# Gate projections of a hybrid decoder step by one level of Strassen's scheme: seven block products for eight

## The chip, the cores and the metric

The kernel runs on one core of one Trainium2 chip. The metric is the device time of one execution in microseconds. Three runs of the kernel before took 2144.91, 2146.51 and 2146.85 us; the median is 2146.51 us.

## The reference

One layer of a decoder for a prompt of 2048 tokens and 8 sample rows (together 2056 columns, `TT`), in float32, with `D_MODEL` 1024:

```python
h = (rms_norm(x, norm_g) * (1.0 + scale) + shift)
proj = h @ w_in                       # columns: q, k, v (1536 each), z_a, u_b, z_b (512 each), g_a, g_b (1024 each)
...                                   # dilated window attention on q, k, v -> a; trailing means of u_b -> p
ya = (a * jax.nn.silu(z_a)) @ w_a_out
yb = (p * jax.nn.silu(z_b)) @ w_b_out
m = jax.nn.sigmoid(g_a) * ya + jax.nn.sigmoid(g_b) * yb
return x + gate * (m @ w_out)
```

The change concerns `g_a` and `g_b`: 2048 of the projection's columns over all 2056 tokens, with a contraction of 1024.

## The kernel before

Float32 accuracy is had with three matmuls where one would do (`three_pass`, L755 to L763): each operand is split into a high part, rounded to TensorE's format, and a low part, the rest; high by high, high by low and low by high are added up in PSUM. Rounding is a copy (a cast on GpSimd or an activation on ScalarE), the low part a subtraction on VectorE.

The program has three stages that follow each other on TensorE: attention with its projections (`attend`, up to about 1160 us), the remaining projections (`finish`), and the outputs (`combine`, from 1764.4 us). The normalised input `h` lies transposed in SBUF as `hH` and `hL`, eight k blocks of 128 rows by 2056 tokens.

`finish` projects 26 tiles of 128 output columns. A tile is five chunks of 412 tokens (the last 408), each of 8 k blocks times 3 matmuls (`project`). Tiles 0 to 7 are u_b and z_b in pairs; between them VectorE makes the window sums (`windows`, L419) and TensorE the pooling matmul of each chunk (`pooled`). Tiles 8 and 9 are z_a, tiles 10 to 25 the gates: `g_a` is eight tiles, `g_b` eight. The weights of a tile are 512 KB, loaded by SyncE (L266) into one of two buffers, rounded by GpSimd (`split_hi`, L381) and subtracted by VectorE (`split_lo`, L397), each at the start of the tile ahead. ScalarE takes every chunk out of PSUM through a Sigmoid (L559) and stores it to `gT_dram`. The work of the 8 sample rows on their cached keys and values runs beside the gate tiles on VectorE: `score` (L453, L455) during tiles 10 to 17, `weigh` (L463) with `values` on TensorE during tiles 20 to 23. The last two tiles are done chunk by chunk in turn (`last`), and beside them the first inputs and weights of `combine` are fetched, rounded and subtracted (`end` on each engine).

`combine` works on 256 tokens at a time: eight branch products (`c_pa`, 256 columns per matmul, two groups of 12), multiplied by the gates on VectorE (L1942, L1944, L1946), then two output products of 512 columns (`c_py`). Its weights come in five pieces by output column (`pieces`, L1790); ScalarE rounds a piece (L1880), VectorE subtracts (L1978), and TensorE waits ahead of a branch product only for the pieces that it reads.

Order is written out by hand. Every engine runs its list in order and waits on semaphores; SyncE's list holds nearly all loads, and its DMAs go out in the order of the list. `wait_ge(proj_done, ...)` waits for a chunk's last matmul, `wait_ge(w_lo, ...)` for a tile's low part.

## Time and profile before

| | |
|---|---|
| median of the runs | 2146.51 us |
| span of the profiled execution | 2144.5 us |
| its own time | not listed apart; the median is 2.0 us above its span |
| TensorE busy | 2099.0 us (98%) |
| VectorE, ScalarE, GpSimd busy | 890.0, 616.0, 243.7 us |
| the sixteen gate tiles | 1398.6 to 1764.4 us |

A busy time is a sum of the instructions' durations without overlap. TensorE's matmuls overlap each other, so the mean duration of one is longer than the distance between two starts. The granted clock in the tables of stretches is a share of full speed. Where a line number is that of a helper (L760 to L762 are the three matmuls of `three_pass`), the names of the tiles tell the use.

### The profile page before, as it was taken

How to read it: one execution, taken by the hardware profiler on the slowest of the kernel's cores; microseconds unless marked ns; L12 is line 12 of the kernel's file. 1: busy time of each engine (PE TensorE's matmuls, PEld its weight loads, DVE VectorE, ACT ScalarE, POOL GpSimd, SP SyncE). 2: the span in 40 equal slices, each digit the busy share in tenths (PEclk: the TensorE clock that was granted, in tenths of full speed). 3: DMA queues.
4: the chain of work that ended last, by engine and by line, in shares of the span. 5: the costliest groups of instructions: out<-in, count | busy, mean ns of one | idle time of the engine just before them, and what ended most of it. 6: DMA issues, size and time to landing. Idle time of an engine off the chain costs nothing.

```text
span 2144.5 us, 36997 instructions
## 1 busy us (share of the span) xinstructions
PE 2099.0 (98%) x12759; PEld 2003.2 (93%) x12759; DVE 890.0 (42%) x2408; ACT 616.0 (29%) x2165; POOL 243.7 (11%) x389
## 2 busy tenths in 40 slices
PE   5999999999999999999999999999999999999999
PEld 3889999999999999999999999999999998998897
DVE  3543333334444344444431244132131247666664
ACT  4634333333333333333354111111121141111010
POOL 2222112111111121111100000000000000000000
PEclk9999999999999999999999999999999999999999
DMA  9756666664645646455244244255422356444441
GB/s 344 256 160 199 221 198 203 207 204 151 201 152 184 196 146 193 151 178 182 89 116 133 83 153 143 94 196 187 152 97 93 126 197 233 169 144 134 149 131 60
DMA packets 258633, 354.05 MB, mean 165 GB/s; under 512 B 24964, under 2 KB 230868, under 8 KB 257069
## 3 DMA queue, kind: packets, MB, share of 16 engines
q1 hardware_dynamic: 209849, 309.82, 43.9%
q10 hardware_dynamic: 48636, 42.33, 6.2%
q8 instruction: 84, 1.38, 0.3%
q14 instruction: 64, 0.52, 0.1%
HBM read 256.52 MB, written 183.77 MB: 205 GB/s over the span
## 4 chain that ended last, share of the span: by engine, by line
PE 92%; DVE 3%; SPq 2%; issue 1%; DMA 1%; ACT 1%; POOL 1%; ACTq 0%; DVEq 0%
PE a_pp L762 13%; PE a_pp L760 13%; PE a_pp L761 12%; PE pp L760 9%; PE pp L762 9%; PE pp L761 9%; PE c_pa L761 3%; PE c_pa L762 3%; PE c_pa L760 3%; PE c_py L761 3%; PE c_py L762 3%; PE c_py L760 2%; PE po L1598 2%; PE pqk L1564 1%; PE po L1597 1%
## 5 line engine op out<-in xcount | busy, mean ns | idle before, releaser
L760 PE MATMUL a_pp<-a_wH,hH 128*128 128x384 f32 x1520 | 528.5, 348 | 6.0 <-DVE qkv L1399 5.2
L762 PE MATMUL a_pp<-a_wH,hL 128*128 128x384 f32 x1520 | 516.2, 340 | 0.0
L761 PE MATMUL a_pp<-a_wL,hH 128*128 128x384 f32 x1520 | 514.2, 338 | 0.0
L760 PE MATMUL pp<-hH,next_H 128*128 128x412 f32 (+1 forms) x1040 | 369.9, 356 | 1.4 <-issue 1.4
L762 PE MATMUL pp<-hH,next_L 128*128 128x412 f32 (+1 forms) x1040 | 363.2, 349 | 0.0
L761 PE MATMUL pp<-hL,next_H 128*128 128x412 f32 (+1 forms) x1040 | 363.1, 349 | 0.0
L760 PEld LDWEIGHTS a_pp<-a_wH,hH 128*128 128x128 f32 x1520 | 287.1, 189 | 10.1 <-ACT qkv L1283 4.4
L761 PEld LDWEIGHTS a_pp<-a_wL,hH 128*128 128x128 f32 x1520 | 287.3, 189 | 0.0
L762 PEld LDWEIGHTS a_pp<-a_wH,hL 128*128 128x128 f32 x1520 | 286.2, 188 | 0.0
L1277 ACT ACTIVATE a_junk<-a_pp 128x128 f32<-128x128 f32 x384 | 106.6, 278 | 545.1 <-PE a_pp L762 539.0
L1388 DVE TENSOR_SCALAR a_ms<-a_ss 128x2 f32<-128x2 f32 (+1 forms) x204 | 34.5, 169 | 524.5 <-ACT a_junk L1277 524.4
L1185 POOL TENSOR_TENSOR a_rs<-a_ms,a_mhalf 128x2 f32<-128x2 f32 (+1 forms) x204 | 140.5, 689 | 842.0 <-DVE a_ms L1388 842.0
L760 PEld LDWEIGHTS pp<-hH,next_H 128*128 128x128 f32 x1040 | 195.6, 188 | 8.6 <-issue 8.1
L761 PEld LDWEIGHTS pp<-hL,next_H 128*128 128x128 f32 x1040 | 195.5, 188 | 3.8 <-issue 3.1
L762 PEld LDWEIGHTS pp<-hH,next_L 128*128 128x128 f32 x1040 | 195.3, 188 | 0.4
L761 PE MATMUL c_pa<-abL,m_wH 128*128 128x256 f32 (+1 forms) x512 | 144.4, 282 | 0.0
L762 PE MATMUL c_pa<-abH,m_wL 128*128 128x256 f32 (+1 forms) x512 | 144.0, 281 | 0.0
L760 PE MATMUL c_pa<-abH,m_wH 128*128 128x256 f32 (+1 forms) x512 | 143.6, 280 | 0.0
L1399 DVE SCALAR_TENSOR_TENSOR qkv<-a_pp,a_rs,gains 128x128 f32<-128x128 f32 x384 | 117.1, 347 | 63.3 <-POOL a_rs L1185 63.2
L559 ACT ACTIVATE ost<-pp 128x412 f32<-128x412 f32 (+1 forms) x80 | 41.3, 516 | 291.1 <-PE pp L762 291.1
L397 DVE TENSOR_TENSOR next_L<-next_st,next_H 128x1024 fp32r<-128x1024 f32 x24 | 29.4, 1224 | 215.3 <-POOL next_H L381 215.3
L1297 ACT ACTIVATE sm<-sm,nm 128x128 f32<-128x128 f32 (+1 forms) x192 | 89.0, 463 | 63.7 <-DVE nm L1420 63.5
(259 smaller groups left out, 3158.2 us busy)
## 6 DMA issues: line engine op xcount, KB each, us to landing
out_dram<-in_state_kv_w_dram SPq DMA_DIRECT2D x64, 1023.5 KB, 5.9
qkv_dram<-qkv SPq DMA_DIRECT2D x192, 192.0 KB, 2.1
qkv_in<-qkv_dram SPq DMA_DIRECT2D x192, 192.0 KB, 2.6
a_wst<-in_w_in_dram SPq DMA_DIRECT2D x38, 512.0 KB, 7.3
gl<-gT_dram SPq DMA_DIRECT2D x64, 264.0 KB, 3.9
out_dram<-in_state_kv_w_dram SPq DMA_DIRECT2D x8, 2044.0 KB, 11.3
gT_dram<-ost ACTq DMA_DIRECT2D x72, 206.0 KB, 2.6
next_st<-in_w_in_dram SPq DMA_DIRECT2D x26, 512.0 KB, 5.6
```

The costliest lines, as they stand in the source:

```text
L397: nc.vector.tensor_tensor(wL[slot], wst[slot], wH[slot].bitcast(F32), ALU.subtract).then_inc(w_lo, 1)
L559: nc.scalar.activation(out, pp[c][:, 0:width(c)], func).then_inc(evac, 1)
L760: nc.tensor.matmul(out, sH, mH, start=(i == 0), stop=False)
L761: nc.tensor.matmul(out, sH, mL, start=False, stop=False)
L762: last = nc.tensor.matmul(out, sL, mH, start=False, stop=(i == len(terms) - 1))
L1185: nc.gpsimd.tensor_tensor(rs[0:rows, s % 2, :], ms[0:rows, s % 2, :], mhalf[0:rows, :], ALU.pow).then_inc(powered, 1)
L1277: nc.scalar.activation(junk[0:rows, :], src[0:rows, i * P:(i + 1) * P], ACT.Square, accum_out=ss[0:rows, s % 2, i:i + 1]).then_inc(squared, 1)
L1297: nc.scalar.activation(sm[:, j % RP, lo:], sm[:, j % RP, lo:], ACT.Exp, bias=nm[:, j % RP:j % RP + 1], accum_out=ot[:, j % RO, E:E + 1]).t ...
L1388: nc.vector.tensor_scalar(ms[0:rows, s % 2, :], ss[0:rows, s % 2, :], 1.0 / E, EPS, ALU.mult, ALU.add).then_inc(meaned, 1)
L1399: done = nc.vector.scalar_tensor_tensor(qkv[0:rows, s % RS, i, :], src[0:rows, i * P:(i + 1) * P], rs[0:rows, s % 2, i:i + 1], gains[0:row ...
L1564: nc.tensor.transpose(pqk[:, 0:P], qkv_in[:, j % RIN, 0, :], ident[:, :])
L1598: nc.tensor.matmul(po[j % 2][:, 0:E], prT[:, j % RP, half(own(j))], qkv_in[:, j % RIN, 2, :], start=not prev, stop=True).then_inc(pv_done, 1)
```

## The change

The product of the gates' weights and `h` is cut once in each direction. Of the weights the two halves are `g_a` and `g_b` (for the same eight f tiles) and the two halves of k; of `h` they are the halves of k and two neighbouring quarters of the tokens (514 columns). Seven products of sums of blocks replace the eight products of blocks, in the form with 15 additions. There are two passes, one for each pair of quarters, and eight steps (f tiles) in each: 16 steps `s` of 7 products `i`. A product is 4 k blocks, 3 matmuls each, over 514 tokens in two halves of 258 columns (two of them twice) in two PSUM banks; three such pairs of banks are used in turn.

- The sums of `h` blocks (T1 to T4) are made once, on GpSimd, in eight units during the pooling tiles (`token_sums`), stored to `comb_dram`, and read back into places of `hH` and `hL` that the pass doesn't need. ScalarE rounds them, VectorE subtracts. Blocks that the second pass needs and the first overwrites are stored to `kept_dram` and read back (`install`).
- The sums of weight blocks are made anew in each step (`weight_sums`): four loads of 256 KB, four GpSimd operations of 512 columns, seven casts, seven subtractions. `w4` has one buffer.
- The outputs are seven additions of 516 columns on VectorE, out of PSUM, and one copy and four Sigmoids on ScalarE, then four stores a step.
- z_a is projected in twelve chunks of 344 or 340 tokens, the upper half of the tokens first.
- The sample rows' work is written into the steps. The weights of `combine` come in eight pieces of 514 columns and half of k; the first four must be ready before its first branch product.

```diff
+    PAIRS, ZA, NF = 4, 2, 10
...
+    QW, SW, HK = TT // 4, 258, KT // 2
...
+    PASSES, GP, NP = 2, KT, 7
+    GS = PASSES * GP
+    K1, K2 = 1, 0
...
+    REGIONS = (((K1, 0), (0, 2), (K2, 0), (0, 3), (1, 2), (1, 3), (K2, 1)),
+               ((K1, 0), (1, 1), (K2, 0), (0, 2), (0, 3), (1, 2), (1, 3)))
+    MADE = {1: T2, 3: T3, 4: T1, 5: T4}
+    KEPT = {0: (K1, 2), 2: (K2, 2), 6: (K2, 3)}
+    UNITS = PASSES * HK
...
+            w4 = sb("w4", [P, NP, HK, P])
+            aH = sb("aH", [P, NP, HK, P], F32R)
+            aL = sb("aL", [P, NP, HK, P], F32R)
+            bank = ps2("g_bank", [P, 6, 512])
...
+        RAW = {0: 0, 2: 1, 3: 2, 5: 3, 4: 4, 1: 5, 6: 6}
+        raw_of = lambda i: w4[:, RAW[i], :, :]
+        u1, u2, u3 = (sums[:, i, :, :] for i in range(3))
+        u4 = u1
...
+        SAW = {1: 1, 2: 2, 3: 3, 4: 5, 5: 6, 6: 7}
+        OUT_OF = {2: 0, 4: 1, 5: 2, 6: 3}
...
+            return (NP * s + i + 2) % 3
...
             def _(sp):
...
+                def store_made(unit):
+                    p, k = divmod(unit, HK)
+                    for n, (which, buf) in enumerate(((T3, 3), (T1, 0), (T2, 1), (T4, 2))):
+                        sp.wait_ge(made_ready, unit * 4 + n + 1)
+                        sp.dma_start(comb_dram[p, which, :, k, :], made[buf][:, :]).then_inc(made_stored, 16)
...
+                def gate_weights(s):
+                    f = s % GP
+                    if s:
+                        sp.wait_ge(g_lo, NP * s)
+                    for i, (c0, kh) in enumerate(((CGA, K1), (CGA, K2), (CGB, K1), (CGB, K2))):
+                        sp.dma_start(w4[:, i, :, :], w_in_v[:, kh * HK:(kh + 1) * HK, c0 + f * P:c0 + (f + 1) * P]).then_inc(g_landed, 16)
+                def install(p, i):
+                    if i in MADE:
+                        sp.dma_start(raw_region(REGIONS[p][i]), comb_dram[p, MADE[i]]).then_inc(t_landed[i], 16)
+                    else:
+                        for part in range(2):
+                            sp.dma_start(as_f32(part, REGIONS[p][i]), kept_dram[i, part]).then_inc(t_landed[i], 16)
...
+                    for s in range(GS):
+                        if s + 1 < GS:
+                            gate_weights(s + 1)
+                        if s + 1 < NS:
+                            keys(s + 1)
+                        if s < NS:
+                            shifted_copy(sp, v, 0, s, bulk)
...
+                        if s == GP - 3:
+                            install(1, 1)
+                        if s == GP - 1:
+                            for i, freed in ((0, 0), (3, 1), (2, 2), (4, 3), (5, 4), (6, 5)):
+                                sp.wait_ge(g_done, NP * s + freed + 1)
+                                install(1, i)
+                        if s == GP:
+                            sp.wait_ge(scored, NS * GROUPS)
+                            for b in range(2):
+                                values(b)
+                            sp.wait_ge(g_done, NP * GP)
+                            load_weights(0)
...
+                        if s == GS - 1:
+                            for i in range(2):
+                                sp.wait_ge(b_stored[i], 16 * PAIRS * NBC // 2)
+                            sp.wait_ge(g_lo, NP * GS)
+                            branch_inputs(0)
+                            for i in range(4):
+                                sp.wait_ge(g_stored[i], 16 * GP)
+                            gates(0, range(4))
+                            for n in range(1, NP + 1):
+                                sp.wait_ge(g_done, NP * s + n)
+                                load_weights(n)
...
             def _(pool):
...
+                def token_sums(unit):
+                    p, k = divmod(unit, HK)
+                    hi = lambda kh, th: hH[:, kh * HK + k, (2 * p + th) * QW:(2 * p + th + 1) * QW].bitcast(F32)
+                    lo = lambda kh, th: hL[:, kh * HK + k, (2 * p + th) * QW:(2 * p + th + 1) * QW].bitcast(F32)
...
+                    if unit:
+                        pool.wait_ge(made_stored, 16 * 4 * unit)
+                    nc.gpsimd.tensor_tensor(d, hi(K2, 1), hi(K1, 1), ALU.subtract)
+                    chained(nc.gpsimd.tensor_tensor(a, lo(K2, 1), lo(K1, 1), ALU.subtract))
+                    nc.gpsimd.tensor_tensor(d, d, a, ALU.add).then_inc(made_ready, 1)
+                    pool.wait_ge(made_ready, unit * 4 + 1)
...
+                    nc.gpsimd.tensor_tensor(c, c, lo(K2, 0), ALU.add).then_inc(made_ready, 1)
...
+                def weight_sums(s):
+                    pool.wait_ge(g_landed, 64 * (s + 1))
+                    if s:
+                        pool.wait_ge(g_lo, NP * s)
+                    nc.gpsimd.tensor_tensor(w4[:, 4, :, :], w4[:, 2, :, :], w4[:, 3, :, :], ALU.add).then_inc(g_sum, 1)
+                    pool.wait_ge(g_sum, 4 * s + 1)
+                    nc.gpsimd.tensor_tensor(w4[:, 2, :, :], w4[:, 0, :, :], w4[:, 2, :, :], ALU.subtract).then_inc(g_sum, 1)
+                    nc.gpsimd.tensor_tensor(w4[:, 5, :, :], w4[:, 4, :, :], w4[:, 0, :, :], ALU.subtract).then_inc(g_sum, 1)
+                    pool.wait_ge(g_sum, 4 * s + 3)
+                    nc.gpsimd.tensor_tensor(w4[:, 6, :, :], w4[:, 1, :, :], w4[:, 5, :, :], ALU.subtract).then_inc(g_sum, 1)
+                    pool.wait_ge(g_sum, 4 * s + 4)
+                def weight_hi(s, i):
+                    if s:
+                        pool.wait_ge(g_done, NP * (s - 1) + i + 1)
+                    nc.gpsimd.tensor_copy(aH[:, i, :, :], raw_of(i)).then_inc(g_hi, 1)
...
+                for n in range(2, NF):
+                    token_sums(n - 2)
...
+                    split_hi(n, n % 2)
+                for s in range(GS):
+                    weight_sums(s)
+                    for i in range(NP):
+                        weight_hi(s, i)
...
             def _(dve):
...
+                def weight_lo(s, i):
+                    dve.wait_ge(g_hi, NP * s + i + 1)
+                    nc.vector.tensor_tensor(aL[:, i, :, :], raw_of(i), aH[:, i, :, :].bitcast(F32), ALU.subtract).then_inc(g_lo, 1)
...
+                def after_product(s, i):
+                    if i == 0:
+                        return
+                    here = product_of(s, i)
+                    dve.wait_ge(g_done, NP * s + i + 1)
+                    if s and i in OUT_OF:
+                        dve.wait_ge(g_stored[OUT_OF[i]], 16 * s)
+                    if i == 1:
+                        dve.wait_ge(act_saw, s + 1)
+                        nc.vector.tensor_tensor(u2, here, u1, ALU.add).then_inc(dve_saw, 1)
+                    if i == 2:
+                        nc.vector.tensor_tensor(out_2(0), here, u1, ALU.add).then_inc(dve_saw, 1)
+                    if i == 3:
+                        dve.wait_ge(dve_saw, SUMS * s + 1)
+                        nc.vector.tensor_tensor(u3, here, u2, ALU.add).then_inc(dve_saw, 1)
+                    if i == 4:
+                        dve.wait_ge(dve_saw, SUMS * s + 3)
+                        nc.vector.tensor_tensor(out_2(1), here, u3, ALU.add).then_inc(dve_saw, 1)
+                        nc.vector.tensor_tensor(u4, here, u2, ALU.add).then_inc(dve_saw, 1)
+                    if i == 5:
+                        nc.vector.tensor_tensor(out_2(2), here, u3, ALU.add).then_inc(dve_saw, 1)
+                    if i == 6:
+                        dve.wait_ge(dve_saw, SUMS * s + 5)
+                        nc.vector.tensor_tensor(out_2(3), here, u4, ALU.add).then_inc(dve_saw, 1)
...
+                    for s in range(GS):
+                        for i in range(NP):
+                            after_product(s, i)
+                            if s < NS and i < GROUPS:
+                                score(s, i)
...
+                            if s == GS - 1:
+                                if i == 1:
+                                    pooling_lo()
...
+                                if i == 3:
+                                    gate_a(1)
+                                    weights_lo(1)
+                                if i == 4:
+                                    attention_lo()
+                                    weights_lo(2)
+                                if i == 5:
+                                    weights_lo(3)
+                            if s + 1 < GS and i >= 3:
+                                for n in range(0 if i == 3 else i, i + 1):
+                                    weight_lo(s + 1, n)
...
             def _(act):
...
+                def after_product(s, i):
+                    p, f = divmod(s, GP)
+                    if i == 0:
+                        act.wait_ge(g_done, NP * s + 1)
+                        if s:
+                            act.wait_ge(dve_saw, SUMS * s)
+                        nc.scalar.activation(u1, product_of(s, i), ACT.Copy).then_inc(act_saw, 1)
+                    if i in OUT_OF:
+                        n = OUT_OF[i]
+                        act.wait_ge(dve_saw, SUMS * s + SUM_OF_OUT[i])
+                        nc.scalar.activation(out_2(n), out_2(n), ACT.Sigmoid).then_inc(g_made, 1)
+                        act.wait_ge(g_made, 4 * s + n + 1)
+                        row, quarter = ((4, 0), (12, 1), (12, 0), (4, 1))[n]
+                        store(n, row + f, 2 * p + quarter)
...
+                            if s == GS - 1:
+                                if i == 1:
+                                    pooling_hi()
+                                if 2 <= i < 5:
+                                    weights_hi(i - 1)
+                                if i == 4:
+                                    attention_hi()
...
             def _(pe):
...
+                def product(s, i):
+                    p = s // GP
+                    if s == 0 and i < 2:
+                        pe.wait_ge(evac, after(Z0 + ZN - 3 + 2 * i))
+                    before = NP * s + i - 3
+                    if before >= 0:
+                        s0, i0 = divmod(before, NP)
+                        if i0:
+                            pe.wait_ge(dve_saw, SUMS * s0 + SAW[i0])
+                        else:
+                            pe.wait_ge(act_saw, s0 + 1)
+                    pe.wait_ge(g_lo, NP * s + i + 1)
+                    if s % GP == 0:
+                        if i in MADE:
+                            pe.wait_ge(t_lo, made_count(p, i))
+                        elif p:
+                            pe.wait_ge(t_landed[i], 32)
+                    rH, rL = region(hH, REGIONS[p][i]), region(hL, REGIONS[p][i])
+                    for j in range(2):
+                        cols = slice(j * (QW - SW), j * (QW - SW) + SW)
+                        done = three_pass(nc, bank[:, 2 * place(s, i) + j, 0:SW],
+                                          [(aH[:, i, k, :], aL[:, i, k, :], rH[:, k, cols], rL[:, k, cols]) for k in range(HK)])
+                    done.then_inc(g_done, 1)
...
+        pieces = ((0, 1), (1, 0), (1, 1), (0, 0), (0, 2), (0, 3), (1, 2), (1, 3))
+        BRANCH_PIECES, OUT_PIECES = 4, (7, 8)
+        LATE_HI, LATE_LO = {1: 4, 3: 5, 4: 6, 5: 7}, {1: 4, 3: 5, 5: 6, KT - 1: 7}
...
+                kh, th = pieces[n]
+                w = (w_a, w_b)[kh] if th < 2 else w_o[:, kh * HK:(kh + 1) * HK, :]
+                start = th % 2 * QW
+                sp.dma_start(piece(w_raw, n), w[:, :, start:min(start + QW, D)]).then_inc(cw_landed[n], 16)
...
-                    pe.wait_ge(cw_lo, piece_of((f + 1) * P - 1) + 1)
+                    pe.wait_ge(cw_lo, BRANCH_PIECES)
```

## Rows read from the trace of the kernel before

**Rows 1.** The page: span, and busy time of each engine

```profile
span 2144.5 us, 36997 instructions
PE 2099.0 (98%) x12759; PEld 2003.2 (93%) x12759; DVE 890.0 (42%) x2408; ACT 616.0 (29%) x2165; POOL 243.7 (11%) x389
```

**Rows 2.** Busy per engine by stretch, then clock, DMA share, GB/s

```profile
1398.60:1764.40 365.80, 365.80 (x1958) 359.56 (x1956) 109.89 (x149) 77.41 (x110) 15.56 (x15) 1.00 0.46 152
```

**Rows 3.** Timeline of TensorE, 412 columns, first and 43rd: start, duration

```profile
1399.28 0.35 PE L760 MATMUL pp<-hH,next_H 128*128 128x412 f32 x1
...
1407.12 0.35 PE L760 MATMUL pp<-hH,next_H 128*128 128x412 f32 x1
```

**Rows 4.** Timeline of TensorE, 256 columns, first, and the 193rd matmul

```profile
1904.50 0.28 PE L760 MATMUL c_pa<-abH,m_wH 128*128 128x256 f32 x1
...
1927.16 0.40 PE L760 MATMUL c_py<-m_wH,mH 128*128 128x512 f32 x1
```

**Rows 5.** Groups by line of GpSimd: count, busy us, mean ns, idle before

```profile
L1185 POOL TENSOR_TENSOR a_rs<-a_ms,a_mhalf 128x2 f32<-128x2 f32 x192 | 132.3, 689 | 791.4 <-DVE a_ms L1388 791.4
L1180 POOL CAST a_wH<-a_wst 128x384 fp32r<-128x384 f32 x96 | 51.1, 539 | 11.4 <-DMA a_wst<-in_w_in_dram 11.4
L381 POOL CAST next_H<-next_st 128x1024 fp32r<-128x1024 f32 x24 | 25.4, 1057 | 527.8 <-PE pp L762 461.7 <-DMA next_st<-in_w_in_dram 66.1
```

**Rows 6.** Groups by line of VectorE

```profile
L1942 DVE TENSOR_TENSOR gm<-c_pa,gl 128x512 f32<-128x512 f32 x56 | 38.5, 687 | 24.6 <-PE c_pa L762 24.6
L453 DVE TENSOR_TENSOR prod<-kt,qb 128x512 f32<-128x512 f32 x24 | 16.6, 691 | 14.2 <-DMA qb<-samp_dram 13.7
L1978 DVE TENSOR_TENSOR m_wL<-m_raw,m_wH 128x3072 fp32r<-128x3072 f32 x4 | 13.4, 3352 | 0.0
...
L419 DVE TENSOR_TENSOR run<-run 128x2061 f32<-128x2061 f32 x3 | 6.9, 2306 | 0.1
```

**Rows 7.** DMA issues: count, KB each, median us from issue to landing

```profile
out_dram<-in_state_kv_w_dram SPq DMA_DIRECT2D x8, 2044.0 KB, 11.3
...
m_raw<-in_w_a_out_dram SPq DMA_DIRECT2D x1, 512.0 KB, 3.9
m_raw<-in_w_b_out_dram SPq DMA_DIRECT2D x1, 512.0 KB, 5.4
```

**Rows 8.** Timeline of SyncE's queue: start and duration of the two issues

```profile
1745.72 0.37 SPq L1790 DMA_DIRECT2D m_raw<-in_w_a_out_dram  x1
1746.13 0.51 SPq L1790 DMA_DIRECT2D m_raw<-in_w_b_out_dram  x1
```

**Rows 9.** Timeline of GpSimd: the seven casts of bl, the first two

```profile
1789.42 5.12 POOL L1824 CAST abH<-bl 128x1056 fp32r<-128x1056 f32 x1 [71.14 <-DMA bl<-bT_dram]
1836.10 1.07 POOL L1824 CAST abH<-bl 128x1056 fp32r<-128x1056 f32 x1 [41.56 <-PE c_pa L762]
```

**Rows 10.** Timeline of VectorE beside these casts, and one subtraction without

```profile
1789.19 4.42 DVE L1978 TENSOR_TENSOR m_wL<-m_raw,m_wH 128x4096 fp32r<-128x4096 f32 x1
...
1793.73 0.83 DVE L737 TENSOR_TENSOR cw<-ol,cw 128x12 f32<-128x12 f32 x1
...
1836.72 0.72 DVE L1946 TENSOR_TENSOR mL<-m,mH 128x256 fp32r<-128x256 f32 x1 [0.48 <-ACT mH L1857]
...
1866.25 0.43 DVE L1946 TENSOR_TENSOR mL<-m,mH 128x256 fp32r<-128x256 f32 x1 [0.48 <-ACT mH L1857]
```

**Rows 11.** Busy by stretch, two stretches with full DMA queues

```profile
1381.00:1385.00 4.00, 4.00 (x24) 3.99 (x23) 0.00 (x0) 0.42 (x1) 0.00 (x0) 1.00 1.04 404
1747.00:1753.00 6.00, 6.00 (x34) 5.99 (x33) 3.22 (x1) 3.02 (x2) 0.00 (x0) 1.00 0.99 324
```

**Rows 12.** Groups by line of ScalarE

```profile
L1880 ACT ACTIVATE m_wH<-m_raw 128x3072 fp32r<-128x3072 f32 x4 | 11.1, 2768 | 0.8 <-ACT ost L595 0.8
L1847 ACT ACTIVATE abH<-a 128x1056 fp32r<-128x1056 f32 x8 | 8.7, 1090 | 92.0 <-DVE a L1920 92.0
```

671 lines of the change are left out of this document (374 added, 297 removed).

## The prediction

> **What bounds the kernel now.** I read the page's first lines, then the table of busy time by stretch, then the timeline of TensorE. TensorE is busy for 2099.0 of 2144.5 us [rows 1]. The stretch that the change rewrites, the sixteen gate tiles, lasts 365.8 us, and TensorE is busy in all of it at a granted clock of 1.00; VectorE has 110 us of work there, ScalarE 77, GpSimd 16 [rows 2]. So only TensorE's work counts there today, and the other engines have room, but room on average: what matters below is how long a chain through them takes.
>
> Of one matmul the profile's duration (349 ns for 412 columns) is not the price, since neighbours overlap; the price is the distance of the starts. With 412 columns 42 matmuls start within 7.84 us, 186.7 ns each [rows 3]. With 256 columns 192 start within 22.66 us, 118.0 ns each [rows 4]. That is 0.453 and 0.461 ns a column: a narrow matmul is hardly dearer per column, and weight loading does not set the pace. Between the two rows a column costs 0.440 ns, so 258 columns are 118.9 ns.
>
> **TensorE's own work.** Removed: 16 tiles x 5 chunks x 24 matmuls = 1920, of which 1536 have 412 columns and 384 have 408 (185.0 ns): 286.8 + 71.0 = 357.8 us. The other 8.0 us of the stretch are the samples' value matmuls, transposes and their seams, and stay. Added: 16 steps x 7 products x 24 matmuls = 2688 of 258 columns: 319.6 us. Gain 38.2 us if nothing waits. The two tiles of z_a become twelve chunks of 344 or 340 columns, 288 matmuls instead of 240: 45.0 against 44.7 us, a loss of 0.3.
>
> **The pooling stage.** GpSimd gets eight units of ten two-input operations of 514 columns, and SyncE 15 MB of stores. A tile of TensorE is 120 matmuls, 22.4 us. At the price taken below a unit is 10 x 1.3 + waits = 14 us, beside one cast of 1.06 [rows 5], and fits. VectorE's window sums of the last pair, five of 2.3 us [rows 6], meet those operations; they have one tile and one chunk (27 us) before the pooling matmul wants them, so some 14 us of slack for at most 14 us of blocking. I take 0; were GpSimd's operation above 2 us, TensorE would wait here too. In the z_a chunks four blocks of 1.05 MB come in, rounded by ScalarE and VectorE; there are 22 us for it and I take 0.
>
> **The loop of the gate steps.** This is the term that decides. One step is 7 x 2.853 = 20.0 us of TensorE. The weights of the next step have one raw buffer (w4), freed only by the last low part of the step before. So each step has a closed loop, none of it on TensorE:
> - SyncE issues four loads of 256 KB. The trace has no such group; two loads of 512 KB, issued 0.41 us apart, land 3.9 and 5.4 us after their issues [rows 7, 8], so 1 MB is there after 5.8 us. Taken 5.9.
> - GpSimd makes four sums of 512 columns. The trace has no large two-input operation of GpSimd. From below: a cast, 539 ns for 384 columns and 1057 for 1024 [rows 5], so 0.64 for 512. From above: reading two operands at the cast's 0.81 ns per column and operand (0.83), on the 0.69 of its two-column operation [rows 5]: 1.52. I take 1.3, nearer the upper row, because the reading of both operands has to be paid and only the fixed part is in doubt. Four with three waits on itself: 5.5.
> - The first cast 0.64, then at product 3 VectorE's first four low parts, each against a cast. Here the two engines block each other: VectorE's subtraction of 4.42 us began at 1789.19, GpSimd's cast at 1789.42 took 5.12 instead of 1.07 and ended 0.93 after it; VectorE's 128x12 operation behind it took 0.83 [rows 9, 10]. In reverse a 0.43 us subtraction took 0.72 beside a cast [rows 9, 10]. So a pair costs 0.45 + 0.55 = 1.0, four of them 4.0, without blocking 2.5.
> - Only then do both sums of product 4 come, 0.69 each [rows 6], which the first product of the next step waits for (it reuses that bank): 1.4.
> - Before the buffer is free: low part, sum, low part, sum, low part: 3.2. Some ten semaphore hops: 0.6.
>
> Together 5.9 + 5.5 + 4.6 + 1.4 + 3.2 + 0.6 = 21.2 us, against 20.0 of TensorE. TensorE then waits 1.2 us once a step, ahead of product 0.
>
> The Trainium skill speaks against the change here. Its "SBUF — State Buffer", section "Who interferes with whom", says that a VectorE instruction with two SBUF inputs and a GpSimd instruction that reads SBUF exclude each other; by that rule, the trace agrees with 5.12 against 1.07. Its "GPSIMD Engine Reference", section "Elementwise — side-by-side cycle accounting", gives 4497 ns for a two-input addition of 2048 columns; scaled to 512 with the cast's fixed part, my estimate is 1.3 us, and the loop would be the same 21.2; no run here shows that price yet.
>
> **Fifteen seams between steps.**
> - Into step 1: its load starts behind six loads of keys: 2.
> - Into steps 2 to 8, seven times 1.2: 8.4.
> - Into step 9: in step 7 the queue carries step 8's weights (1.0 MB), a state copy of 0.5 MB read and written (2.8 us from 11.3 for 2 MB [rows 7]), nine blocks of 1.05 MB for the second pass, three stores of 0.26 MB, then step 9's weights: 12.3 MB at the 324 to 404 GB/s that full queues move [rows 11], 34 + 2.8 us from 4.5 us into step 7. They land 20 us into step 8; then 5.5 + 4.6 + 1.4 + 0.6. Step 9 starts at 32 instead of 20: 12.
> - Into steps 10 to 14: the weighing of values, five two-input operations of 0.69 [rows 6], runs up to twice a step on VectorE and blocks GpSimd's sums, and value matmuls wait for their loads: 2.5 each, 12.5.
> - Into step 15: two group sums of about 5 us with their exponentials stand before the low parts: 6.
>
> Sum 40.9. The stretch becomes 319.6 + 8.0 + 40.9 = 368.5 against 365.8: +2.7.
>
> **Into the last stage.** Before, TensorE passed from the gates to the branch matmuls without a gap, as the output weights came in column pieces. Now the first branch matmul needs four whole pieces. In step 15 SyncE issues 2.1 MB of inputs, then pieces 1 to 3 (3.1 MB): 5.2 MB in 15 us from 3 on, the third there at 18. ScalarE rounds it in 1.9 (2.77 for 3072 columns [rows 12]) and only then the attention rows, 1.09 [rows 12]; VectorE follows with 1.25, a low part of 2.3 (3.35 for 3072 [rows 6]), a sum 0.7 and the last low part 2.3. That is 28, and TensorE is done at 20: 8. It cannot be below 0, and 12 if the queues move the lower rate of rows 11. Inside the last stage VectorE starts late but the four banks cover it: 0.
>
> Sum against the profiled execution: 2144.5 + 2.7 + 0.3 + 8 = 2155.5. The median of the runs is 2146.5, 2.0 above the span; with these 2157.5, taken as **2157 us**.
>
> **Rivals.**
> 1. The loop fits. Its condition is a GpSimd sum near the cast, 0.64, or no blocking. Then 5.9 + 2.9 + 3.2 + 1.4 + 3.2 + 0.6 = 17.2, hidden. The queue at the pass change still costs 8, the value steps 3, the group sums 3, the end 8: 2146.5 - 38.2 + 0.3 + 22 = 2131. For it: the average load is far below the span. Against: the blocking in [rows 9, 10]. If these 22 are hidden too: 2109.
> 2. The loop is longer. GpSimd's sum at 1.52 and landings 1 us later, since ScalarE's four stores per step share the queues: +1.9 a seam, 28 in all: 2185. For it: landings of the trace grow with what is in flight. Above 2 us GpSimd would also bound the pooling stage.
> 3. The forecast, which ends slower; the first rival ends faster. The point between them is a loop of 20.0: at a sum of 1.0 the plain steps no longer wait, and 1.2 less at each of the fourteen later seams brings the time to 2141; the time of before is met near 1.1.
>
> **Chances.** Forecast 0.52, first rival 0.27, all hidden 0.05, longer loop 0.16. A run tells 0.2% (4.3 us): faster, below 2142.2, is 0.32 with the first two and the edge of the loop; between, 0.13, are sums of 1.0 to 1.15; slower 0.55. The likeliest case's own range is 2147 to 2170. For 8 in 10: 2125, just under the first rival, to 2187.
>
> **What would show it.** Right: starts of product 0 are 21 to 22 us apart in steps 2 to 8, with a wait on VectorE ahead of it; GpSimd's 128x512 sums at 1.2 to 1.4; step 8 lasts over 30; TensorE idles 6 to 12 us before the first branch matmul. Wrong: steps of 20.0, with only seams 8 and 14 wider (first rival); steps above 23 (second); matmuls of 258 columns more than 121 ns apart, which [rows 4] speak against; or waits in the pooling stage.

## The result, and the profile after

The changed kernel takes 2218.81 us (four runs, 2215.34 to 2221.21) against 2145.71 us of the kernel before on the same chip: ratio 1.0339, 95% interval 1.0325 to 1.0354. The forecast was 2157, with 2125 to 2187 for the range: the direction was right, the size was not.

First the page of the kernel after; the rows answer to [rows 1].

```profile
span 2216.9 us, 38614 instructions
PE 2097.0 (95%) x13575; PEld 1992.0 (90%) x13575; DVE 1084.0 (49%) x2627; ACT 624.2 (28%) x2166; POOL 522.2 (24%) x629
```

TensorE is busy only 2.0 us less than before, though 38 us of matmuls were to be saved, and the span is 72.4 us longer: part of its matmuls ran at a lower clock, and there is idle time. The table of stretches says where. Columns: stretch, its length, busy of PE, PEld, DVE, ACT, POOL with their instructions, granted clock, DMA share, GB/s. It answers to [rows 2]; below it two single steps.

```profile
1397.20:1834.90 437.70, 362.86 (x2723) 349.00 (x2721) 273.73 (x357) 78.10 (x104) 171.38 (x165) 0.92 0.65 179
1477.05:1503.67 26.62, 21.94 (x167) 21.74 (x166) 14.95 (x21) 3.15 (x6) 10.89 (x11) 0.87 0.62 164
1503.67:1525.87 22.20, 21.01 (x176) 20.81 (x175) 13.81 (x20) 3.14 (x6) 10.89 (x11) 1.00 0.72 183
```

The stretch of the gates, up to the first branch matmul, went from 365.8 to 437.7 us: 71.9 of the 72.4. It began 1.4 us earlier than before, so the pooling and z_a stages cost nothing; the last stage went from 380.1 to 382.0. TensorE idles for 74.8 us in it, and the granted clock fell from 1.00 to 0.92: after most of its gaps the next matmuls run at the lower of its two levels (0.42 us for 258 columns instead of 0.28).

Whom it waits for, from the view of waits (total us, times, longest):

```profile
PE g_bank L1072 <- DVE sums L709: 43.6, 12, 8.1
PE ppool L955 <- DVE kt L660: 8.9, 3, 3.6
PE c_pa L1072 <- DVE m_wL L2298: 8.6, 1, 8.6
PE g_bank L1072 <- ACT sums L869: 4.9, 1, 4.9
```

The main wait is the forecast's: the first product of a step wants the bank that the sums of product 4 free. To see what those sums wait for, one step is followed through the queues in the timeline (start, duration, engine, line; idle before in brackets).

```profile
1475.33 0.38 ACTq L860 DMA_DIRECT2D gT_dram<-out  x1
1475.75 0.68 DVE L682 TENSOR_TENSOR aL<-w,aH 128x512 fp32r<-128x512 f32 x1
1476.46 2.34 SPq L395 DMA_DIRECT2D w<-in_w_in_dram  x4
1476.53 0.42 ACTq L860 DMA_DIRECT2D gT_dram<-out  x1
1487.18 1.29 POOL L553 TENSOR_TENSOR w<-w 128x512 f32<-128x512 f32 x1 [13.94 <-DMA w<-in_w_in_dram]
...
1491.16 1.29 POOL L558 TENSOR_TENSOR w<-w 128x512 f32<-128x512 f32 x1
1492.51 5.78 POOL L565 CAST aH<-w 128x512 fp32r<-128x512 f32 x7
1493.16 4.11 DVE L682 TENSOR_TENSOR aL<-w,aH 128x512 fp32r<-128x512 f32 x4 [7.19 <-POOL aH L565]
1497.19 0.68 DVE L708 TENSOR_TENSOR out<-g_bank,sums 128x516 f32<-128x516 f32 x1
1497.79 0.68 DVE L709 TENSOR_TENSOR sums<-g_bank,sums 128x516 f32<-128x516 f32 x1
...
1498.53 0.58 PE L1072 MATMUL g_bank<-hH,aH 128*128 128x258 f32 x1 [4.68 <-DVE sums L709]
...
1500.80 0.68 DVE L682 TENSOR_TENSOR aL<-w,aH 128x512 fp32r<-128x512 f32 x1
1501.58 0.42 ACTq L860 DMA_DIRECT2D gT_dram<-out  x1
```

From the last low part of one step (it ends at 1476.43) to the last of the next (1501.48) is a ring: each member waits for the one before it. Only one member came out far from the forecast:

| member of the ring | forecast | this step |
|---|---|---|
| last low part ends (1476.43) to SyncE's issue (1476.46) | in the hops, 0.6 for all | 0.03 |
| issue to GpSimd's first sum | 5.9 | 10.7 |
| four sums to the first cast | 5.5 | 5.3 |
| cast, and four low parts against casts | 4.6 | 4.7 |
| two sums of product 4 | 1.4 | 1.2 |
| low, sum, low, sum, low (ends 1501.48) | 3.2 | 3.1 |
| together | 21.2 | 25.05 |

The ring's 25.05 us are the step itself (25.1 on average below), and TensorE is no member. The expectations below put the ring at 26.2 or "about 26", 1.2 too long, since they took the low part before the last, which ends at 1475.23, for the last. The landing (issue of the four loads to the first sum) was 10.5, 10.3, 10.7, 9.2, 10.7 and 9.7 us in the loads issued in steps 1 to 6. Near the issue stand ScalarE's stores of finished gate tiles: three of them in each of these steps, 2.9 and 1.1 us before the issue and 0.1 after it. The groups of GpSimd over the whole run, which answer to [rows 5], say that its sums had the price that was taken:

```profile
L553 POOL TENSOR_TENSOR w<-w 128x512 f32<-128x512 f32 x16 | 20.8, 1303 | 241.7 <-DMA w<-in_w_in_dram 241.7
L565 POOL CAST aH<-w 128x512 fp32r<-128x512 f32 x112 | 96.9, 907 | 16.7 <-PE g_bank L1074 15.7
```

### The profile page after: what moved, and what is told of

Same layout as the page of the kernel before. It is cut to its first block, busy times and chain, and to the rows that moved or that the text cites. A ratio compares the mean times of both kernels' runs of the same rounds, so it can differ in the third digit from the quotient of the medians.

```text
span 2216.9 us, 38614 instructions
## 1 busy us (share of the span) xinstructions
PE 2097.0 (95%) x13575; PEld 1992.0 (90%) x13575; DVE 1084.0 (49%) x2627; ACT 624.2 (28%) x2166; POOL 522.2 (24%) x629
## 4 chain that ended last, share of the span: by engine, by line
PE 75%; DVE 8%; DMA 6%; POOL 4%; SPq 3%; issue 2%; ACT 1%; ACTq 0%; DVEq 0%; POOLq 0%
PE a_pp L1074 12%; PE a_pp L1072 12%; PE a_pp L1073 12%; DMA w<-in_w_in_dram 4%; PE pp L1072 3%; PE pp L1074 3%; PE pp L1073 3%; PE c_py L1072 3%; PE c_pa L1073 3%; PE c_py L1073 3%; PE c_py L1074 3%; PE c_pa L1072 2%; PE c_pa L1074 2%; DVE aL L682 2%; PE po L1913 2%
## 5 line engine op out<-in xcount | busy, mean ns | idle before, releaser
L1072 PE MATMUL g_bank<-hH,aH 128*128 128x258 f32 x896 | 267.4, 298 | 55.1 <-DVE sums L709 43.6
L1073 PE MATMUL g_bank<-hL,aH 128*128 128x258 f32 x896 | 263.7, 294 | 0.0
L1074 PE MATMUL g_bank<-hH,aL 128*128 128x258 f32 x896 | 263.2, 294 | 0.0
L1072 PEld LDWEIGHTS g_bank<-hH,aH 128*128 128x128 f32 x896 | 180.8, 202 | 66.9 <-DVE sums L709 46.2
L1073 PEld LDWEIGHTS g_bank<-hL,aH 128*128 128x128 f32 x896 | 180.8, 202 | 0.0
L1074 PEld LDWEIGHTS g_bank<-hH,aL 128*128 128x128 f32 x896 | 180.5, 201 | 0.0
L1072 PE MATMUL pp<-hH,next_H 128*128 128x412 f32 (+3 forms) x416 | 148.8, 358 | 1.4 <-issue 1.4
L1074 PE MATMUL pp<-hH,next_L 128*128 128x412 f32 (+3 forms) x416 | 142.4, 342 | 0.0
L1073 PE MATMUL pp<-hL,next_H 128*128 128x412 f32 (+3 forms) x416 | 142.3, 342 | 0.0
```

Source lines behind the costliest of these rows:

```text
L1072: nc.tensor.matmul(out, sH, mH, start=(i == 0), stop=False)
L1073: nc.tensor.matmul(out, sH, mL, start=False, stop=False)
L1074: last = nc.tensor.matmul(out, sL, mH, start=False, stop=(i == len(terms) - 1))
```

## The experiments

Time is a median of four runs; the ratio stands to the kernel before timed together with it (2144.9 to 2146.5 us). "Step" is the mean distance of ScalarE's copies of product 0 from step 1 to step 7, from the timeline; in the changed kernel it is 25.1. Four runs leave out work that the result needs (less work, without sums, weights once, no stores); they only show what that work costs.

| run | time us | ratio, interval | step us |
|---|---|---|---|
| e1_filler | 2215.82 | 1.0330 (1.0313 to 1.0347) | 24.8 |
| e18_filler20 | 2217.03 | 1.0333 (1.0312 to 1.0353) | 24.8 |
| e17_less_work | 2216.74 | 1.0336 (1.0319 to 1.0353) | 24.7 |
| e2_nosums | 2156.46 | 1.0052 (1.0035 to 1.0069) | 20.3 |
| e5_once | 2130.02 | 0.9925 (0.9908 to 0.9941) | 20.1 |
| e4_order | 2207.08 | 1.0287 (1.0269 to 1.0304) | 24.2 |
| e14_dve_sums | 2198.44 | 1.0244 (1.0227 to 1.0261) | 23.9 |
| e6_actcast | 2229.16 | 1.0394 (1.0377 to 1.0411) | 25.5 |
| e3_keys | 2214.63 | 1.0328 (1.0311 to 1.0346) | 24.0 |
| e9_two_loads | 2222.63 | 1.0354 (1.0337 to 1.0371) | 25.5 |
| e10_no_stores | 2175.79 | 1.0134 (1.0118 to 1.0151) | 22.4 |
| e13_late_stores | 2185.63 | 1.0189 (1.0172 to 1.0206) | 22.7 |
| e7_early | 2180.60 | 1.0164 (1.0147 to 1.0181) | 21.5 |
| e8_all | 2182.55 | 1.0172 (1.0151 to 1.0193) | 20.7 |
| e11_order_early | 2168.68 | 1.0102 (1.0085 to 1.0119) | 20.5 |
| e12_queue | 2165.60 | 1.0097 (1.0080 to 1.0113) | 21.2 |
| e15_all | 2186.96 | 1.0193 (1.0176 to 1.0210) | 22.4 |
| e16_best | 2160.34 | 1.0071 (1.0053 to 1.0089) | 20.4 |

### Is it the ring, or TensorE and its clock?

**A filler ahead of the first product.**

```diff
+                    if s in (1, 2, 3, 4, 5, 6, 7, 10, 11, 12, 15) and i == 0:
+                        for n in range(40):
+                            nc.tensor.matmul(ppool[0][:, 0:256], hH[:, n % KT, 0:P], hH[:, n % KT, 0:256],
+                                             start=True, stop=True)
```

> Eleven of the fifteen seams between gate steps get 40 extra matmuls of 256 columns (about 4.7 us at full clock) just ahead of the first product, where TensorE idles in the changed kernel; nothing else is touched. Loop theory: the step's period is set by a ring that TensorE is not in (load of the weights, four GpSimd sums, casts and low parts, sums of product 4, last low parts: about 26 us), so the stretch stays at 437.7 +- 4 us and the run at 2219 +- 5, while the half-clock time in the filled steps nearly vanishes. Clock theory: the 35 us that the half clock costs TensorE stand in the time, so about 11/16 of it comes back: 2195 to 2202. If the granted clock stays low without idle in front of it, the clock has another cause than the idle.

Measured 2215.8. The filled steps, as stretches of the filler run:

```profile
1475.97:1500.86 24.89, 24.89 (x210) 24.89 (x209) 14.54 (x21) 3.15 (x6) 10.89 (x11) 1.00 0.67 170
1500.86:1525.74 24.88, 24.88 (x210) 24.88 (x209) 14.27 (x20) 3.14 (x5) 10.90 (x11) 1.00 0.73 181
```

TensorE is never idle, the clock is 1.00, and the step is still 24.9: where the gap is filled, the half clock is gone. But the run can't say more. 20.1 and 4.8 us of filler are 24.9, so TensorE is itself the bound there: the filler was longer than the average gap (43.6 us over 15 seams, 2.9). Two runs mend that.

**Less work on TensorE** (from step 1 on, the products with `i < 3` leave out their pass over the low part of `h`), and **a filler of 20**.

```diff
+                        if s and i < 3:
+                            for k, (sH, sL, mH, mL) in enumerate(terms):
+                                nc.tensor.matmul(out, sH, mH, start=(k == 0), stop=False)
+                                done = nc.tensor.matmul(out, sL, mH, start=False, stop=(k == HK - 1))
```

> From the second step on, products 0 to 2 leave out the pass over the low half of the tokens: 24 of 168 matmuls a step, 2.9 us at full clock and more at half. Loop theory: TensorE is not in the ring, so the steps stay where they are: stretch 430 to 440, run 2212 to 2222, with 2.9 us more idle a step. Clock theory (TensorE's own matmuls, some at half speed, set the step): 15 times 2.9 or more come off: 2165 to 2180.

> The first filler was longer (4.8 us) than the idle of an average seam (2.9), so that TensorE itself filled the whole step of 24.9 and the run could not show less. Here it is 20 matmuls, 2.4 us, in the same eleven steps, and TensorE needs 22.4 a step. Loop theory: steps of 24.5 to 25.5 as before, run 2212 to 2220. Clock theory: the steps go to 22.5 to 23.5 as the half clock goes: 2195 to 2203.

Both runs (2216.7 and 2217.0) stay where the changed kernel was, with steps of 24.7 and 24.8. The waits of the run with less work:

```profile
PE g_bank L1007 <- DVE sums L709: 61.2, 12, 7.1
PE ppool L955 <- DVE kt L660: 16.8, 3, 6.4
```

Some 43 us of matmuls (15 steps of 2.9) were taken away, the run changed by 2 us, and the saved time went into longer waits (61.2 for 43.6, 16.8 for 8.9) and, for the rest, into more matmuls at the lower clock (0.87 for 0.92 on average over the stretch). So TensorE isn't in the ring of the plain steps, and the half clock costs nothing there: slow matmuls fill a gap that is there anyway.

**Without GpSimd's sums**, and **weights once** (its loads, sums, casts and low parts of the steps from 1 on are taken out).

```diff
                     if s:
                         pool.wait_ge(g_lo, NP * s)
+                        return
```
```diff
-                        if s + 1 < GS:
-                            gate_weights(s + 1)
...
-                    pe.wait_ge(g_lo, NP * s + i + 1)
+                    pe.wait_ge(g_lo, i + 1)
```

> GpSimd's four sums of weights are left out from the second gate step on (the products then use the sums of step 0). Loop theory: the ring loses 5.3 us, 26.2 to 20.9, so 14 or 15 seams shrink by 5 each: stretch 365 to 375, run 2142 to 2156, granted clock near 1.00. Rival, the sums are not on the ring (blocking or TensorE's own matmuls at the lower clock set the step): under 25 us gained, over 2194.

> The weights of the gates are loaded, summed and split once, before step 0, and every step uses those of step 0 (left out: the loads, sums, casts and low parts of fifteen steps). Loop theory: nothing but TensorE is left in the plain steps, so they are 20.0 to 20.1 us apart; the pass change keeps some 8 us (its installs), and the wait of the first branch matmul stays at 8.7: stretch 335 to 345, run 2115 to 2127, granted clock 1.00. Rival, a good part of the seams of steps 9 to 14 (22 to 24 us in the run without sums) belongs to the weighing of the values and not to the ring: these steps stay above 22 and the run above 2135.

Without sums: 2156.5, 62 us less, at the upper edge of the expected range, steps of 20.3. By the table above the ring is near 19.7 (25.05 less 5.3), under TensorE's 20.1, so TensorE has become the bound. With no loads, sums, casts and low parts: 2130.0, steps of 20.10, and one of them as a stretch, with one that holds value matmuls, then the whole of the gates:

```profile
1440.87:1460.97 20.10, 20.10 (x170) 20.10 (x169) 8.63 (x13) 3.15 (x5) 0.00 (x0) 1.00 0.65 160
1657.50:1679.91 22.41, 22.41 (x174) 20.42 (x173) 11.15 (x18) 3.15 (x6) 0.00 (x0) 1.00 0.26 83
```

```profile
1397.20:1746.95 349.75, 336.56 (x2726) 327.60 (x2725) 176.41 (x252) 78.17 (x104) 0.00 (x0) 0.98 0.61 178
```

20.10 us over 168 matmuls are 119.6 ns each, against 118.9 forecast. The expectation of 2115 to 2127 was missed by 3: the stretch keeps 349.7, not 345. Its last wait, 6.3, is that of the first branch matmul. And 2130 is what the first rival gave for a ring that fits (2131).

### Which member is what it costs?

**Low parts after the sums of product 4.**

```diff
-                            if s + 1 < GS and i >= 3:
-                                for n in range(0 if i == 3 else i, i + 1):
+                            if s + 1 < GS and i >= 4:
+                                for n in range(0 if i == 4 else i, i + 1):
```

> VectorE starts the next step's low parts after the sums of product 4 instead of before them (five at once, then one after each of the last two products). Loop theory: the ring loses the two sums of product 4 (1.3 us) and gains nothing, since the low parts still follow GpSimd's casts: steps of about 25, run 2195 to 2205. Rival, the wait of TensorE's first product on product 4's bank (43.6 us in 12 waits) is itself what sets the time: that wait goes, and 40 us with it, 2175 to 2185.

2207.1, a gain of 12 where the ring promised 14 to 24 and the bank's wait 40. TensorE's longest wait is now another: 18.9 us in 9 waits on `aL`. The wait of 43.6 us was worth 12, since behind it in the same ring stood the next.

**The four sums on VectorE** (GpSimd waits on `g_sum` and casts).

```diff
+                            if s + 1 < GS and i == 3:
+                                dve_sums(s + 1)          # waits on g_landed, then the four sums
                             if s + 1 < GS and i >= 3:
```

> From the second step on the four sums of weights run on VectorE (0.69 us each) just ahead of its low parts, casts stay on GpSimd. Loop theory: 5.3 us of the ring become 2.8 to 3.0: steps of about 23.8, run 2180 to 2188; every microsecond taken from a member of the ring shows 14 times. Rival, VectorE is then the bound, since it stands at the landing with sums of products 4 to 6 behind it: 2200 or more.

2198.4: 20 us instead of 31 to 39, above the expected range and just under the rival's 2200. The four sums take 2.74 us in VectorE's timeline, so 2.5 less in the ring, but the step shrank by 1.2. One line of VectorE's waits says why:

```profile
DVE w L691 <- DMA w<-in_w_in_dram: 8.4, 4, 4.1
```

Only four of the fifteen groups of sums waited for the landing. The other eleven began 0.3 to 4.8 us after it, since in VectorE's list they stand behind the sum of product 3, for which VectorE waits on TensorE, and behind the sample rows' work.

**Casts on ScalarE.**

```diff
+                            if s + 1 < GS and i >= 3:
+                                for n in range(0 if i == 3 else i, i + 1):
+                                    cast(s + 1, n)       # nc.scalar.activation(aH, raw_of(n), ACT.Copy)
```

> From the second step on the seven casts aH run on ScalarE, at the place in its order where VectorE has the low parts; GpSimd has only the four sums. Blocking theory: cast and low part no longer exclude each other, four pairs cost 2.5 to 2.8 instead of 4.0 us, VectorE's low part is 0.45 to 0.6 instead of 0.89 on average; ring 26.2 to about 24.7, run 2194 to 2202. Rival, what is saved is lost again since the copy of product 0, the sigmoids and the stores stand behind the casts on ScalarE: 2212 or more.

2229.2, slower by 10: the rival came true. VectorE's timeline of this run shows both halves of it:

```profile
1492.35 2.50 DVE L682 TENSOR_TENSOR aL<-w,aH 128x512 fp32r<-128x512 f32 x4 [6.89 <-ACT aH L885]
...
1497.30 0.69 DVE L682 TENSOR_TENSOR aL<-w,aH 128x512 fp32r<-128x512 f32 x1 [1.24 <-ACT aH L885]
...
1503.58 0.69 DVE L682 TENSOR_TENSOR aL<-w,aH 128x512 fp32r<-128x512 f32 x1 [1.85 <-ACT aH L885]
```

Four low parts take 2.50 us instead of 4.11: the blocking between VectorE and GpSimd was priced right. But the last three casts stand behind a sigmoid and a store each on ScalarE, so the low parts 4 to 6 are 3.1 us apart instead of 1.2. In the same step the landing was only 6.7 us (1479.72 to 1486.39 in SyncE's and GpSimd's timelines): spread out by the casts, the last stores were issued at 1474.71 and 1477.86, ahead of the loads.

### Why does 1 MB take 10 us?

**Keys later**, **two loads of 512 KB**, and **no stores**.

```diff
                         if s + 1 < NS:
+                            sp.wait_ge(g_landed, 64 * (s + 2))
                             keys(s + 1)
```
```diff
-                    for i, (c0, kh) in enumerate(((CGA, K1), (CGA, K2), (CGB, K1), (CGB, K2))):
+                    for i, c0 in ((0, CGA), (2, CGB)):     # one load each into w4[:, i:i + 2], all eight k blocks
```
```diff
+                        if s in (0, 8):
                             store(n, row + f, 2 * p + quarter)
+                        else:
+                            act.sem_inc(g_stored[n], 16)
```

> In steps 0 to 6 SyncE issues the keys of the next sample only once the four weight loads have landed. Queue-sharing theory: landing falls from 10.6 to about 7 us from the issue in those steps, seven seams shrink by 3.5: 2195 to 2200. Rival, the landing is the price of 1 MB in four loads beside the stores of the gates (in step 13 there were no keys and it took 9.7): landing above 9 us, 2212 to 2220, and late keys may add a wait of VectorE on the ring.

> The weights of a step come as two loads of 512 KB (both k halves of a gate) instead of four of 256 KB; the slots are renamed to fit, the rest is as changed. In the changed kernel 10.2 us pass in the middle from SyncE's first issue to GpSimd's first sum, where 5.9 were forecast. If the number of loads is the reason (2.3 us of issues instead of 0.9 or less): 8.7 to 9.2, ring and steps 1.2 less, run 2198 to 2206. If what else is in the queues, or the rate of the transfers themselves, is the reason: still 9.9 or more, run 2212 to 2219.

> ScalarE's stores of gate tiles are left out in all steps but 0 and 8, and the last stage reads the tile of these two in place of all eight. Traffic theory: the stores (1 MB a step, in pieces of 1028 bytes) share the queues with the weights; without them the weights are there 7 to 7.5 us after the issue instead of 10.2, steps of 23, run 2170 to 2182. Rival, the landing is the price of the loads themselves: 9 us or more, run over 2203.

Keys: landings of 8.6 to 9.8 (mean 9.2), run 2214.6: one microsecond of the ten is theirs, and the queue-sharing theory in the form "it is the keys" falls. Two loads: landings of 9.8 to 11.4, run 2222.6, no gain. Without stores (the last stage then reads the gate tiles of steps 0 and 8 in place of all): 43 us less, 2175.8. **Stores later** then asks whether it is their bytes or their moment:

```diff
-                        store(n, row + f, 2 * p + quarter)
+                        held.append((n, row + f, 2 * p + quarter))
+                        if n < 2 or s in (GP - 1, GS - 2, GS - 1):
+                            while held: store(*held.pop(0))
...
+                    if i == 1 and held:
+                        act.wait_ge(g_landed, 64 * (s + 2))
+                        while held: store(*held.pop(0))
```

> No byte is left out: ScalarE holds back the last two stores of a step (products 5 and 6) until the weights that are on their way have landed (not in steps 7, 14 and 15). Timing theory: these two stores of 257 KB stand in the queues together with the weights; with them behind it the weights land 7 to 8 us after the issue instead of 10.2, run 2175 to 2190, near the run without stores (2176). Rival, the amount counts and not the moment (stores, keys and copies keep the queues full at any time), or ScalarE held at the wait delays the sigmoids: over 2205.

2185.6, 33 us less with every byte still stored. The DMA issues of the same stretch (1425 to 1560 us) in the changed kernel, without stores and with late stores (count, KB each, median us from issue to landing):

```profile
w<-in_w_in_dram SPq DMA_DIRECT2D x24, 256.0 KB, 7.4
```
```profile
w<-in_w_in_dram SPq DMA_DIRECT2D x24, 256.0 KB, 4.1
```
```profile
w<-in_w_in_dram SPq DMA_DIRECT2D x24, 256.0 KB, 4.1
```

A load lands in 7.4, 4.1 and 4.1 us; from the issue of the four to the first sum it is 10.2, 6.3 to 7.4 (the loads issued in steps 2 to 7) and 6.2 to 8.0 (steps 0 to 5; in step 6, beside an install of 1 MB, 10.4). Steps 2 to 5 without stores are 20.1 to 21.5 us long by the copies, where 21.2 was forecast. In the step above two stores were issued within 1.2 us of the loads (1475.33 and 1476.53 against 1476.46), and not by chance: VectorE waits for the first cast, so the outputs of products 4, 5 and 6 come in one burst right before the last low part that frees the buffer. The Trainium skill, "DMA: Bandwidth & Descriptors", section "Queues, rings and completion order", says that a DMA engine goes round its queues packet by packet; by that, loads in flight together with stores take longer, which agrees with 7.4 against 4.1 us. The stores don't show the converse: their median is 6.1 us in the changed kernel and 7.2 when two of a step are held back.

**Slots loaded one by one.**

```diff
-                    if s:
-                        sp.wait_ge(g_lo, NP * s)
                     for i, (c0, kh) in enumerate(...):
+                        if s:
+                            sp.wait_ge(g_lo, NP * (s - 1) + (1, 3, 4, 6)[i])
```

> Each of the four raw slots is loaded again as soon as its own low part is done (after low parts 0, 2, 3 and 5) instead of all four after low part 6. Loop theory: three loads start about 5 us sooner and the fourth 1.2, so only one load of 256 KB (some 6 us) stands in the ring instead of four (10): ring 26.2 to 21.5, steps of 21 to 22.5, run 2150 to 2170. Rival, the landing is set by what else is in the queues (stores of the gates, copies, keys), not by the four loads themselves: steps of 24 or more, over 2195.

2180.6, 38 us less. The plain steps came as expected (21.5, for 21 to 22.5), the run did not (2150 to 2170): the seams into steps 7, 8, 9 and 15 keep 25.5, 33.8, 27.1 and 29.9 us.

### Together

The edits are those above: e8_all is order, slots and casts on ScalarE; e11_order_early order and slots; e12_queue adds three moved loads (diff); e15_all adds the sums on VectorE to e12_queue, e16_best the late stores.

```diff
+                gate_weights(1)
                 keys(0)
...
-                        if s + 1 < GS:
+                        if s + 1 < GS and s not in (0, GP, GP + 6):
                             gate_weights(s + 1)
...
+                                if i == 6:
+                                    gate_weights(s + 2)      # step 9's, ahead of the last install
...
                         if s == GP + 5:
+                            gate_weights(s + 2)              # step 15's, ahead of the attention rows
                             sp.wait_ge(aTs_ready, 1)
```

> Three edits together: low parts after the sums of product 4, casts on ScalarE, slots loaded one by one. Loop theory: the ring falls below TensorE's 20.0 or close to it in the plain steps; the pass change, the steps with values and the first branch matmul keep what they have in the run without sums: 2135 to 2155. Rival, the gains overlap, since the ring then closes through ScalarE (casts behind sigmoids and stores): above 2165.

> Slots loaded one by one as in the run that gave 2181, and low parts after the sums of product 4 as in the run that gave 2207, casts left on GpSimd. Loop theory: the two edits shorten different parts of the ring, and the run of three edits lost through ScalarE's casts what it won by the order (casts alone had cost 10): 2166 to 2174. Rival, in the plain steps the ring is no longer the bound (20 to 21 us apart already), so the order has nothing left to give: 2178 to 2186.

> As the run before, and three issues of weights moved ahead in SyncE's order: step 1's ahead of the first keys, step 9's ahead of the last install of the pass change, step 15's ahead of the loads of attention rows. Queue theory: seams into steps 1, 9 and 15 stood 7.3, 9.5 and 8.9 us above the run without any loads; they lose 4 to 6 each, 12 to 16 in all: 2152 to 2160. Rival, the transfers put back (installs, attention rows) are then what is late: within 4 us of the run before. In neither case does it beat the kernel before (2145 to 2147), since 22 to 25 us of the value steps and of the first branch matmul remain.

> Low parts after the sums of product 4, slots loaded one by one, three loads moved ahead in SyncE's order, and the four sums on VectorE. Loop theory: the plain steps are at 20 already, so only the seams of the pass change, of steps 9 to 12 and of step 15 shorten, by 1 to 2.5 each: 2150 to 2160. Rival, the sums come after product 4 now and put 2.8 us ahead of the low parts that TensorE's next product waits for: over 2163. Neither beats the kernel before.

> Low parts after the sums of product 4, slots loaded one by one, three loads moved ahead in SyncE's order (2166 together), and the last two stores of a step held back until the weights have landed. Loop theory: the plain steps stay at 20; the seams into steps 9 to 12 and 15, 2 to 7 us each, lose what their landings lose, 8 to 14 in all: 2150 to 2158. Rival, with slots loaded one by one the loads are spread over the step and the held stores only push ScalarE's sigmoids back: 2164 or more. It does not reach the kernel before in either case.

Order and slots alone give 2168.7. With casts on ScalarE as well it was 2182.6, where 2135 to 2155 was expected: 14 us of the miss are that edit, and without it the range is still missed by 14. Three loads moved ahead give 3 more (2165.6, intervals overlap), not 12 to 16. The sums on VectorE lose 21 (2187.0): behind the sums of product 4 they close another ring, and this one holds TensorE. Product 4 comes first, then its two sums, the four sums of weights, five low parts, the sum of product 5 that frees the bank of the next step's product 1 (TensorE waits there 13 times, 16.0 us in all), and products 1 to 4. The plain steps are 22.2 apart. With the stores late it is 2160.3, between the expected 2150 to 2158 and the rival's 2164, and its interval overlaps that of e12_queue. Alone the late stores had given 33 us and here 5, so the moment of the stores and the buffer filled as a whole are largely the same microseconds. The stretch of this last one:

```profile
1397.20:1773.85 376.65, 344.97 (x2721) 333.73 (x2720) 274.92 (x357) 77.99 (x104) 173.04 (x165) 0.96 0.79 209
```

No run here that does all the work beats the kernel before. Even weights once, with nothing of the ring left, keeps only 16 us of the 38 that the matmuls were to save; the first rival's other 22 are mostly the pass change and the wait of the first branch matmul.

## Why the prediction was right or wrong

**What failed: the landing.** The step is "SyncE issues four loads of 256 KB ... Taken 5.9." It was 10.2. The 1 MB that it came from [rows 7, 8] had one store of 206 KB beside it, issued at 1746.33, after the loads, and the trace has it in packets of 1024 bytes. In this kernel three stores of 257 KB go out in the 3 us around the issue, and the packets of the loads have 512 bytes. With the stores away the landing was 6.3 to 7.4, with two of them late 6.2 to 8.0, so some 3 to 4 us are theirs. What is left over 5.9 may be the smaller packets; no run tests that. The hops were not too small: SyncE issues 0.03 us after the low part that it waits for. The second rival named the stores, but priced them at 1 us.

**Where the missing 61 us are.** The stretch from the first gate matmul to the first branch matmul, by copies of product 0. The forecast's 8.0 us of other work stand in the row into 10 to 14; a step's forecast is 20.0 and its seam.

| | forecast | measured | no stores | weights once |
|---|---|---|---|---|
| to product 0 of step 0 | 2.9 | 5.9 | 6.1 | 5.7 |
| into 1 | 22.0 | 24.9 | 25.6 | 17.5 |
| into 2 to 7 | 127.2 | 150.4 | 134.4 | 120.6 |
| into 8 and 9 | 53.2 | 64.5 | 55.8 | 49.5 |
| into 10 to 14 | 120.5 | 131.4 | 118.9 | 110.8 |
| into 15 | 26.0 | 30.2 | 25.5 | 20.9 |
| to the first branch matmul | 25.1 | 30.5 | 29.4 | 24.4 |
| sum | 376.9 | 437.7 | 395.6 | 349.4 |

Each of the seams 2 to 7 is 3.9 over, the landing's 4.3 less what the hops and other members gave back. The seams 8 to 15 are over by 26 in all, and the run without stores takes 26 away (200.2 for 226.0), so these too are the stores'; late stores do most of it (208.4). The run without stores keeps 7 us over in 2 to 7; 6 of them are in the seam into 2, whose loads meet the stores of step 0, which this run still has.

The forecast has no term for two smaller things. The first copy of product 0 is 3 us late in all three runs: in the changed kernel ScalarE first waits until its last store of z_a has landed, at 1402.77. No wait of TensorE comes of it, and the 3 us belong to the row below, where TensorE's first gap is 5.1 us for 2 forecast. And at the pass change TensorE waited 4.9 us (up to 1614.86) for ScalarE's copy of product 0 of step 8, which stood behind the rounding of a sum block that landed only at 1612.40; with weights once this wait is 6.4.

**What was right.** 258-column matmuls at 118.9 ns: 119.6. GpSimd's sum at 1.3: 1.29 where nothing is beside it, 1.30 to 1.59 in the means. Four low parts against casts, 4.0: 4.03 (1493.16 to 1497.19). The ring itself, its order and the wait on the sums of product 4: as drawn, and with the stores away the ring took 22.2, 21.2, 21.2 and 21.5 us in steps 2 to 5, for the forecast's 21.2. Step 8 above 30: 38.6 by the starts of product 0. Pooling stage 0: the gates began 1.4 us early. Wait of the first branch matmul, 8: 8.6. The branch "steps above 23 (second)" is what came, at 2219 instead of 2185, outside the range.

**What was not in the forecast at all.** The granted clock. The gaps bring it to the lower level, and TensorE is busy for 362.9 us in the stretch against 336.6 with weights once. Read from the busy times this looks like 26 us of the loss. The runs with less work and with the short filler show that in the plain steps it isn't: the ring sets the step and the slow matmuls lie in its slack. It costs time where TensorE is the bound again right after a gap: the first 27 branch matmuls ran 0.41 instead of 0.28 us and took 5.9 us where 118 ns each would be 3.2, and the last stage is 1.9 us longer.

## What to carry to other kernels

When a change adds a chain that starts and ends at one buffer, add its members up as a ring, and take the transfer's time from rows in which transfers of the same shape and the same stores are in flight at the same moment: ask which stores the engines release just before the buffer comes free. A ring that is 1 us over the bound costs 1 us per step, and shortening any member gains only until the next bound, which can be another ring; the wait that the profile names (43.6 us here) is not the gain (12). Before you blame a lower clock, take work from the engine: if the time stays, the engine was waiting anyway.

## What was unexpected in the hardware

- A 256 KB load took 7.4 us in the median with three stores of 257 KB near its issue and 4.1 with two of these stores held back until the loads had landed. Halving the number of loads (two of 512 KB) did not help: 10.7 us to the first sum on average against 10.2.
- From the end of VectorE's last low part to the start of SyncE's first issue, which waits for it, only 0.03 us pass (1476.43 to 1476.46).
- Four subtractions of VectorE took 4.11 us with GpSimd's casts of the same size beside them, and 2.50 with those casts on ScalarE.
